# A retention layer's recurrence products as three products of rounded parts, with the query decay applied on the way out of PSUM

## The chip, the cores and the metric

The kernel runs on one core of one Trainium2 chip. The metric is the device time of one execution in microseconds (us).

## The reference

A block of two layers on a sequence of 1024 rows of 1024 floats is followed by a second block; the change touches only the first layer of the first block, a retention layer with 4 heads, keys and queries of width 256 and values of width 512, in chunks of 128 rows:

```python
log_gamma = jnp.log(1.0 - 2.0 ** (-5.0 - jnp.arange(h, dtype=jnp.float32)))
idx = jnp.arange(c, dtype=jnp.float32)
intra_decay = ...  # exp((i - j) * log_gamma) where i >= j, else 0
q_decay = jnp.exp((idx + 1.0)[:, None] * log_gamma[None, :])
k_decay = jnp.exp((c - 1.0 - idx)[:, None] * log_gamma[None, :])
chunk_decay = jnp.exp(c * log_gamma)
k = k * dk ** -0.5

def step(state, inp):
    qc, kc, vc = inp
    scores = jnp.einsum('bihd,bjhd->bhij', qc, kc) * intra_decay[None]
    intra = jnp.einsum('bhij,bjhe->bihe', scores, vc)
    inter = jnp.einsum('bihd,bhde->bihe', qc, state) * q_decay[None, :, :, None]
    new_state = (state * chunk_decay[None, :, None, None]
                 + jnp.einsum('bjhd,bjhe->bhde', kc * k_decay[None, :, :, None], vc))
    return new_state, intra + inter
```

The output is then normalised by row, multiplied by silu(gate), and projected; its input is an RMS norm of x times a weight of 1024 by 6144.

## The kernel before

The work is written by hand for five engine queues; semaphores order them. `retain` is the stage in question. After the normed input stands transposed in SBUF (`hT`), a loop runs over the 4 heads. Each head has three passes over 8 tiles of 128 rows: pass 0 projects query and key (512 columns) and VectorE rotates them into `rot`; pass 1 projects the values and ScalarE copies them into `v`; pass 2 projects the gate and runs the recurrence, one chunk a tile.

Every projection (`products`, line 91) is made of three products of rounded parts: both operands are split into a high part in the type fp32r and a low part, the rest in fp32r, and high times high, low times high and high times low are summed in PSUM. A split of a matrix costs a ScalarE copy (high, line 407) and a VectorE subtraction (low, line 477). The products of the recurrence have plain fp32 operands instead.

In pass 2 TensorE does, for tile t: four transposes of `rot` (line 366) into the bank `p_tr`; the first half of the gate projection (12 products); the scores (line 372, 128 by 128); the state's update `p_kv` = decayed keys by values (line 380, two products of 512 columns, not for the last tile); the second half of the gate (12 products); the output `p_o` = masked scores by values (line 387) plus decayed queries by state (line 392, two, not for the first tile).

Around it, ScalarE copies the transposed queries and keys from `p_tr` to `qkT` (line 455), makes silu of the gate (459), issues the store of the tile before, squares the output with a row sum (465), and divides (467). GpSimd decays the keys (302) and the queries (310) and takes the root (316). VectorE masks the scores (556), updates the state once the output product of the tile is done (563, 566), and writes the gated output (573). The queues also carry the splits of the next weights, four 128x512 pieces at a time: the second half of the gate's weights at the very end of pass 1 (they need the last value projection done), the next head's first half after the fifth tile of pass 2 (t == 4), its second half after the last. On VectorE and ScalarE each instruction waits behind the one before it, and `split_next(1, 1)` is the last step of both before tile 0 of pass 2.

Of the kernel before, what the change touches and what calls it, by code (L numbers as in the profile page):

```python
# [22 lines left out]
P = 128  # L23
# [76 lines left out]
class Mem:  # L100


    def __init__(self, nc, ctx, prefix):
        self.nc, self.ctx, self.prefix = nc, ctx, prefix
        self.signals = []
        ctx.callback(self.clear_signals)

    def sb(self, name, *shape, dt=F32):
        return self.ctx.enter_context(self.nc.sbuf_tensor(f"{self.prefix}_{name}_sb", list(shape), dt))

# [73 lines left out]
def retain(nc, ident, dram, early, hT, w_first, w_second, o_dram):  # L184
# [9 lines left out]
    with ExitStack() as ctx:  # L194
# [3 lines left out]
        v = mem.sb("v", P, TILES, RET_V)  # L198
        g_col = mem.sb("g_col", P, KT)
# [7 lines left out]
        qdT = mem.sb("qdT", P, 2, 2, P)  # L207
        k_dec = mem.sb("k_dec", P, 2, RET_QK)
        gate = mem.sb("gate", P, 2, RET_V)
        scoresT = mem.sb("scoresT", P, 2, P)  # L210
        state = mem.sb("state", P, 2, RET_V)
        o_junk = mem.sb("o_junk", P, RET_V)
# [12 lines left out]
        row_factors = [scoresT[:, b, :] for b in range(2)]  # L225
# [16 lines left out]
        (qkT_tr, qkT_copied, s_done, masked, kdec_done, qdT_done, kv_done, state_done, o_done) = mem.sems(  # L242
            "qkT_tr", "qkT_copied", "s_done", "masked", "kdec_done", "qdT_done", "kv_done", "state_done", "o_done")
# [7 lines left out]
        def block_number(head, c, per, plus):  # L251

            return head.times(PASSES * per, c * per + plus)

# [30 lines left out]
        def _(pool):  # L285
# [8 lines left out]
            with pool.Fori(0, RET_HEADS) as h:  # L294
                head = Place(h, 1, 0)

                def decay_keys(t):

                    pool.wait_ge(rot_done, head.times(TILES, t + 1))
                    if t >= 2:  # L300
                        pool.wait_ge(kv_done, head.times(2 * (TILES - 1), 2 * (t - 1)))
                    pool.tensor_tensor(k_dec[:, t % 2, :], rot[:, t, RET_QK:], k_decay.broadcast_to([P, RET_QK]), ALU.mult).then_inc(kdec_done, 1)

                pool.wait_ge(tab_in, head.times(16, 16))
                decay_keys(0)
                for t in range(TILES):
                    if t >= 1:

                        pool.wait_ge(qkT_copied, head.times(TILES, t + 1))
                        pool.tensor_tensor(qdT[:, t % 2], qkT[:, t % 2, 0:2, :],  # L310
                                           q_decay.rearrange("p (a n) -> p a n", a=1).broadcast_to([P, 2, P]), ALU.mult).then_inc(qdT_done, 1)
                    if t + 1 < TILES - 1:
# [2490 lines left out]
```

## Time and profile before

| | |
|---|---|
| median of three runs | 2470.94 us (2467.70 to 2477.11) |
| the profiled execution | 2472.37 us |
| its span in the profile | 2470.6 us |
| granted TensorE clock, mean | 0.973 |
| TensorE busy (matmuls) | 2320.0 us, 94% |
| VectorE, ScalarE, GpSimd busy | 1020.8, 827.5, 237.6 us |
| the four passes 2 | about 82 us each, from about 132, 291.5, 451 and 610.5 us |

The profiled execution's own time is 1.8 us over the span. A matmul's length in the profile covers its way through the array, and lengths overlap; what a matmul costs in a row of them is the distance between two starts. PE is TensorE, PEld its weight loads, DVE VectorE, ACT ScalarE, POOL GpSimd. In a timeline "x4" is four instructions merged, and a number in brackets is the idle time before, with what ended it.

### The profile page before, as it was taken

Reading aid. Unit: us, or ns where it says so; the run is one execution under the profiler, and the core shown is the slowest. Engines: PE = TensorE matmul, PEld = TensorE weight load, DVE = VectorE, ACT = ScalarE, POOL = GpSimd, SP = SyncE. Lnnn points to the kernel's source line nnn. Section 1 sums busy time; section 2 is a strip of 40 time slices with the busy share of each in tenths; the row PEclk is TensorE's granted clock in tenths of the full one; section 3 lists DMA queues with packets and bytes.
Section 4 is the critical chain, followed back from the end, with each engine's and each line's share of the span. In section 5 each row is a group of like instructions: output and inputs, shape, how many; then the busy total and the mean of one; then the engine's idle time right before and its main releaser. Section 6 shows DMA issues by size and latency. Waiting matters only on the chain. (4 is left out here: it accounts for less than half of the span.)

```text
span 2470.6 us, 33196 instructions
## 1 busy us (share of the span) xinstructions
PE 2320.0 (94%) x11754; PEld 1812.7 (73%) x11754; DVE 1020.8 (41%) x2882; ACT 827.5 (33%) x2132; POOL 237.6 (10%) x371
## 2 busy tenths in 40 slices
PE   6999999999979997999989799989999999699998
PEld 5877867768758886677767686767777677688876
DVE  4323224123224114355443325666565666533342
ACT  4121221221223113455543224544444544423232
POOL 1010010010010000122110000010010100101013
PEclk9999999999989998999999899999999999899999
DMA  3111111111126113011133501110111102333322
GB/s 139 37 51 51 59 49 49 55 42 57 42 93 239 68 60 128 7 50 50 48 107 112 180 14 58 58 42 23 44 43 60 41 9 75 93 107 112 102 94 86
DMA packets 125301, 175.12 MB, mean 71 GB/s; under 512 B 7577, under 2 KB 73177, under 8 KB 123617
## 3 DMA queue, kind: packets, MB, share of 16 engines
q1 hardware_dynamic: 119088, 157.39, 18.9%
q10 hardware_dynamic: 6064, 15.84, 1.7%
q8 instruction: 82, 1.34, 0.2%
q14 instruction: 67, 0.54, 0.1%
HBM read 143.79 MB, written 29.42 MB: 70 GB/s over the span
## 5 line engine op out<-in xcount | busy, mean ns | idle before, releaser
L91 PE MATMUL heads_p_ps<-ret_w_second_hi_sb,ret_hT_hi_sb 128*128 128x512 f32 x384 | 161.6, 421 | 0.0
L91 PE MATMUL heads_p_ps<-ret_w_second_lo_sb,ret_hT_hi_sb 128*128 128x512 f32 x384 | 149.9, 390 | 0.0
L91 PE MATMUL heads_p_ps<-ret_w_second_hi_sb,ret_hT_lo_sb 128*128 128x512 f32 x384 | 149.4, 389 | 0.0
L91 PE MATMUL att_proj_ps<-br_w_second_hi_sb,br_hT_hi_sb 128*128 128x512 f32 x272 | 117.2, 431 | 2.9 <-DVE br_w_second_lo_sb L2096 2.9
L91 PE MATMUL att_proj_ps<-br_w_second_lo_sb,br_hT_hi_sb 128*128 128x512 f32 x272 | 106.9, 393 | 0.0
L91 PE MATMUL att_proj_ps<-br_w_second_hi_sb,br_hT_lo_sb 128*128 128x512 f32 x272 | 106.5, 392 | 0.0
L2056 ACT ACTIVATE br_x_sb<-br_x_sb,att_max_neg_sb 128x256 f32<-128x256 f32 (+7 forms) x128 | 97.8, 767 | 15.5 <-DVE att_max_neg_sb L2269 15.4
L566 DVE SCALAR_TENSOR_TENSOR heads_state_sb<-heads_state_sb,heads_tab_sb,heads_kv_ps 128x512 f32<-128x512 f32 x48 | 33.7, 744 | 161.0 <-PE heads_o_ps L392 161.0
L91 PEld LDWEIGHTS heads_p_ps<-ret_w_second_hi_sb,ret_hT_lo_sb 128*128 128x128 f32 x384 | 72.2, 188 | 20.9 <-issue 6.7
L91 PEld LDWEIGHTS heads_p_ps<-ret_w_second_hi_sb,ret_hT_hi_sb 128*128 128x128 f32 x384 | 72.1, 188 | 20.6 <-issue 6.7
L459 ACT ACTIVATE heads_gate_sb<-heads_p_ps 128x512 f32<-128x512 f32 x32 | 19.1, 597 | 196.4 <-PE heads_p_ps L91 196.4
L91 PEld LDWEIGHTS heads_p_ps<-ret_w_second_lo_sb,ret_hT_hi_sb 128*128 128x128 f32 x384 | 72.1, 188 | 15.7
L2466 PE MATMUL mrg_b_ps<-mrg_w_br_hi_sb,mrg_yT_hi_sb 128*128 128x256 f32 x256 | 74.0, 289 | 9.2 <-DVE mrg_w_br_lo_sb L2627 8.1
L2535 ACT ACTIVATE mrg_yT_hi_sb<-br_y_raw_sb 128x1024 fp32r<-128x1024 f32 x32 | 33.9, 1060 | 140.1 <-PE mrg_b_ps L2466 119.9
L91 PE MATMUL swa_p_ps<-swa_w_first_hi_sb,swa_hT_hi_sb 128*128 128x512 f32 x160 | 70.5, 441 | 10.5 <-DVE swa_qn_sb L1352 7.0
L91 PE MATMUL att_proj_ps<-br_w_fox_hi_sb,br_hT_hi_sb 128*128 128x512 f32 x144 | 64.9, 451 | 12.1 <-ACT att_vz_fox_sb L1953 8.8
L1886 PEld LDWEIGHTS att_t_ps<-all_ident_sb,br_x_sb 128*128 128x128 f32 x432 | 48.1, 142 | 37.0 <-issue 24.0
L2466 PE MATMUL mrg_b_ps<-mrg_w_br_lo_sb,mrg_yT_hi_sb 128*128 128x256 f32 x256 | 73.0, 285 | 0.0
L2466 PE MATMUL mrg_b_ps<-mrg_w_br_hi_sb,mrg_yT_lo_sb 128*128 128x256 f32 x256 | 73.0, 285 | 0.0
L1886 PE MATMUL att_t_ps<-all_ident_sb,br_x_sb 128*128 128x128 f32 x432 | 69.2, 286 | 3.8 <-DVE br_x_sb L2284 1.9
L407 ACT ACTIVATE ret_w_second_hi_sb<-early_w_kv_sb 128x512 fp32r<-128x512 f32 x52 | 28.5, 620 | 126.8 <-PE heads_p_ps L91 126.8
L2649 DVE TENSOR_TENSOR mrg_sig_sb<-mrg_b_ps,mrg_sig_sb 128x512 f32<-128x512 f32 x32 | 22.0, 689 | 112.3 <-PE mrg_b_ps L2466 112.3
(448 smaller groups left out, 6274.3 us busy)
## 6 DMA issues: line engine op xcount, KB each, us to landing
early_w_kv_sb<-a_w_blocks SPq DMA_DIRECT2D x28, 1024.0 KB, 5.4
all_w_block_sb<-w_turns SPq DMA_DIRECT2D x12, 2048.0 KB, 9.4
br_y_raw_sb<-branch_yT_dram SPq DMA_DIRECT2D x32, 512.0 KB, 4.2
ret_o_dram<-early_x_rows_sb ACTq DMA_DIRECT2D x32, 256.0 KB, 2.4
all_w_block_sb<-swa_turns SPq DMA_DIRECT2D x4, 2048.0 KB, 10.0
ret_out_o_rows_sb<-ret_o_dram ACTq DMA_DIRECT2D x6, 1024.0 KB, 5.2
x_dram<-early_x_rows_sb SPq DMA_DIRECT2D x12, 512.0 KB, 3.3
heads_v_sb<-x SPq DMA_DIRECT2D x8, 512.0 KB, 4.1
```

Source lines behind the costliest of these rows:

```text
L91: mm = pe.matmul(out, rows[a], w[b], start=(k == 0 and a + b == 0), stop=(k == KT - 1 and b == 1))
L407: act.activation(w_at(kind)(k)[0], w_raw[:, k % HALF, :], ACT.Copy).then_inc(w_hi, 1)
L459: act.activation(gate[:, b, :], p_proj[b][:], ACT.Silu).then_inc(gate_done, 1)
L566: dve.scalar_tensor_tensor(state[:, k, :], state[:, k, :], chunk_decay, p_kv[k][:], ALU.mult, ALU.add).then_inc(state_done, 1)
L1886: tr = pe.transpose(p_tr[b][:, j * P:(j + 1) * P], probs[:, t % 2, a, (lo + j) * P:(lo + j + 1) * P], ident[:])
L2056: act.activation(part, part, ACT.Exp, bias=max_neg[:, t % 2, a:a + 1], scale=SCALE, accum_out=p_sum[:, t % 2, a:a + 1]).then_inc(exp_done, 1)
L2466: mm = pe.matmul(p_br[b][:, n * QW:(n + 1) * QW], rows[i], w[j], start=(k + i + j == 0), stop=(k == PAIRS - 1 and j == 1))
L2535: act.activation(y_parts[t % 2][0][:], y_raw[:, t % RAWS], ACT.Copy).then_inc(y_hi, 1)
L2649: dve.tensor_tensor(sig[:, t % 2, :], p_br[t % 2][:], sig[:, t % 2, :], ALU.mult).then_inc(prod_done, 1)
```

## The change

All products of the recurrence with 512 columns are made of three products of rounded parts (`three`). For this the values, the decayed keys, the decayed queries, the masked scores and the state are split: the high part on ScalarE (`value_high`, `key_high`, `state_high`, the query copy), the low part on VectorE; the high part of the scores is VectorE's too, by a second masking. GpSimd keeps only the root. The transposed queries go to the bank `p_s` beside the scores, and VectorE multiplies them by the decay as it takes them out (`decay_queries`); the scores are made of the decayed queries, and the table that masks them takes that decay out again. ScalarE copies only the keys. The state's update no longer waits for the tile's output product, since that product reads the parts and not the state; it waits for ScalarE's copy of the state's high part. The scores remain fp32 products. The low part of the values lies over the values.

```diff
+        v_low = mem.over("v", "v_low", P, TILES, RET_V, dt=F32R)
+        v_high = mem.sb("v_high", P, 2, RET_V, dt=F32R)
...
+        def three(pe, out, rows, w, first, last):
+
+            for a, b in ((0, 0), (1, 0), (0, 1)):
+                mm = pe.matmul(out, rows[a], w[b], start=first and a + b == 0, stop=last and b == 1)
+            return mm
...
-                pe.wait_ge(qkT_copied, head.times(TILES, t + 1))
+                pe.wait_ge(kT_copied, head.times(TILES, t + 1))
+                pe.wait_ge(qd_done, head.times(TILES, t + 1))
...
+                    pe.wait_ge(v_lo, head.times(TILES, t + 1))
                     if t < TILES - 1:
-                        pe.wait_ge(kdec_done, head.times(TILES - 1, t + 1))
+                        pe.wait_ge(kd_lo, head.times(TILES - 1, t + 1))
...
                         for k in range(2):
-                            pe.matmul(p_kv[k][:], k_dec[:, b, k * P:(k + 1) * P], v[:, t, :],
-                                      start=True, stop=True).then_inc(kv_done, 1)
+                            three(pe, p_kv[k][:], [part[:, b, k * P:(k + 1) * P] for part in k_dec], v_parts(t),
+                                  True, True).then_inc(kv_done, 1)
...
-                    pe.wait_ge(masked, head.times(TILES, t + 1))
+                    pe.wait_ge(sc_lo, head.times(TILES, t + 1))
...
-                    mm = pe.matmul(p_o[b][:], scoresT[:, b, :], v[:, t, :], start=True, stop=(t == 0))
+                    mm = three(pe, p_o[b][:], [part[:, b, :] for part in scoresT], v_parts(t), True, t == 0)
                     if t >= 1:
-                        pe.wait_ge(qdT_done, head.times(TILES - 1, t))
-                        pe.wait_ge(state_done, head.times(2 * (TILES - 1), 2 * t))
+                        pe.wait_ge(qd_lo, head.times(TILES - 1, t))
+                        pe.wait_ge(st_lo, head.times(2 * (TILES - 1), 2 * t))
                         for k in range(2):
-                            mm = pe.matmul(p_o[b][:], qdT[:, b, k, :], state[:, k, :], start=False, stop=(k == 1))
+                            mm = three(pe, p_o[b][:], [part[:, b, k, :] for part in qdT], [part[:, k, :] for part in state_parts],
+                                       False, k == 1)
...
+                act.wait_ge(tab_in, head.times(16, 16))
+                value_high(0)
+                key_high(0)
                 split_next(1, 1)
                 for t in range(TILES):
                     b = t % 2
                     act.wait_ge(qkT_tr, head.times(TILES, t + 1))
-                    act.activation(qkT[:, b], p_tr[:].rearrange("p (k n) -> p k n", k=4), ACT.Copy).then_inc(qkT_copied, 1)
+                    act.activation(qkT[:, b, 2:4], p_tr[:, 2 * P:4 * P].rearrange("p (k n) -> p k n", k=2), ACT.Copy).then_inc(kT_copied, 1)
+                    if t >= 1:
+                        act.wait_ge(qd_done, head.times(TILES, t + 1))
+                        act.activation(qdT[0][:, b], qkT[:, b, 0:2], ACT.Copy).then_inc(qd_hi, 1)
+                    if t + 1 < TILES:
+                        value_high(t + 1)
+                    if t + 1 < TILES - 1:
+                        key_high(t + 1)
...
                     act.activation(o_ms[:, b:b + 1], o_ssq[:, b:b + 1], ACT.Copy, scale=1.0 / RET_V, bias=EPS).then_inc(oms_done, 1)
+                    if t < TILES - 1:
+                        state_high(t)
...
                 split_next(0, 1)
                 split_next(1, 0)
+                dve.wait_ge(tab_in, head.times(16, 16))
+                value_low(0)
+                key_low(0)
                 split_next(1, 1)
-                dve.wait_ge(tab_in, head.times(16, 16))
+                decay_queries(0)
                 for t in range(TILES):
                     b = t % 2
 
+                    if t >= 1:
+                        dve.wait_ge(qd_hi, head.times(TILES - 1, t))
+                        dve.tensor_tensor(qdT[1][:, b], qkT[:, b, 0:2], full(qdT[0])[:, b], ALU.subtract).then_inc(qd_lo, 1)
                     dve.wait_ge(s_done, head.times(TILES, t + 1))
...
+                    if t + 1 < TILES:
+                        value_low(t + 1)
+                    if t + 1 < TILES - 1:
+                        key_low(t + 1)
 
                     if t < TILES - 1:
-                        dve.wait_ge(o_done, head.times(TILES, t + 1))
...
+                        decay_queries(t + 1)
+                        for k in range(2):
+                            dve.wait_ge(st_hi, head.times(2 * (TILES - 1), 2 * t + k + 1))
+                            dve.tensor_tensor(state_parts[1][:, k, :], state[:, k, :], full(state_parts[0])[:, k, :], ALU.subtract).then_inc(st_lo, 1)
```

On VectorE, at the start of pass 2 before the change (line 477 with `second` is the low half of the gate's last weights, 556 the first masking; register rows stand between):

```order
106 L477 TENSOR_TENSOR ret_w_second_lo_sb<-early_w_kv_sb,ret_w_second_hi_sb 128x512 [waits heads_w_hi]
107 L528 REGISTER_ALU
108 L477 TENSOR_TENSOR ret_w_second_lo_sb<-early_w_kv_sb,ret_w_second_hi_sb 128x512 [waits heads_w_hi]
109 L528 REGISTER_ALU
110 L477 TENSOR_TENSOR ret_w_second_lo_sb<-early_w_kv_sb,ret_w_second_hi_sb 128x512 [waits heads_w_hi]
111 L528 REGISTER_ALU
112 L477 TENSOR_TENSOR ret_w_second_lo_sb<-early_w_kv_sb,ret_w_second_hi_sb 128x512 [waits heads_w_hi]
113 L556 TENSOR_TENSOR heads_scoresT_sb<-heads_s_ps,heads_tab_sb 128x128 [waits heads_s_done,heads_tab_in]
```

The same place on VectorE with the change:

```order
105 L588 TENSOR_TENSOR heads_v_low_sb<-heads_v_sb,heads_v_high_sb 128x512 [waits heads_v_hi,heads_tab_in]
106 L592 ISA
107 L593 SCALAR_TENSOR_TENSOR heads_k_dec_lo_sb<-all_w_block_sb,heads_tab_sb,heads_k_dec_hi_sb 128x256 [waits heads_kd_hi]
108 L565 REGISTER_ALU
109 L514 TENSOR_TENSOR ret_w_second_lo_sb<-early_w_kv_sb,ret_w_second_hi_sb 128x512 [waits heads_w_hi]
110 L565 REGISTER_ALU
111 L514 TENSOR_TENSOR ret_w_second_lo_sb<-early_w_kv_sb,ret_w_second_hi_sb 128x512 [waits heads_w_hi]
112 L565 REGISTER_ALU
113 L514 TENSOR_TENSOR ret_w_second_lo_sb<-early_w_kv_sb,ret_w_second_hi_sb 128x512 [waits heads_w_hi]
114 L565 REGISTER_ALU
115 L514 TENSOR_TENSOR ret_w_second_lo_sb<-early_w_kv_sb,ret_w_second_hi_sb 128x512 [waits heads_w_hi]
116 L599 TENSOR_TENSOR heads_qkT_sb<-heads_s_ps,heads_tab_sb 128x256 [waits heads_qkT_tr]
```

Two subtractions stand ahead of the four of the weights now, and the decay of the first queries, for which TensorE's scores wait, stands behind them.

On ScalarE, inside pass 2 (second tile) before the change (the squares of one tile, then the copy of the next tile's transposes):

```order
62 L465 ACTIVATE heads_o_junk_sb,heads_o_ssq_sb<-heads_o_ps 128x512 [waits heads_o_done]
63 L467 ACTIVATE heads_o_ms_sb<-heads_o_ssq_sb 128x1 [waits heads_o_sq]
64 L455 ACTIVATE heads_qkT_sb<-heads_tr_ps 128x512 [waits heads_qkT_tr]
65 L459 ACTIVATE heads_gate_sb<-heads_p_ps 128x512 [waits heads_g_done]
66 L442 ISA [waits heads_gated]
67 L442 DMA ret_o_dram<-early_x_rows_sb 128x512
```

And with the change:

```order
67 L500 ACTIVATE heads_by_sin_sb,heads_o_ssq_sb<-heads_o_ps 128x512 [waits heads_o_done]
68 L502 ACTIVATE heads_o_ms_sb<-heads_o_ssq_sb 128x1 [waits heads_o_sq]
69 L466 ISA
70 L467 ACTIVATE heads_state_hi_sb<-heads_state_sb 128x512 [waits heads_state_done]
71 L466 REGISTER_ALU
72 L467 ACTIVATE heads_state_hi_sb<-heads_state_sb 128x512 [waits heads_state_done]
73 L483 ACTIVATE heads_qkT_sb<-heads_tr_ps 128x256 [waits heads_qkT_tr]
74 L486 ACTIVATE heads_qdT_hi_sb<-heads_qkT_sb 128x256 [waits heads_qd_done]
75 L454 ACTIVATE heads_v_high_sb<-heads_v_sb 128x512 [waits heads_v_copied]
76 L461 ACTIVATE heads_k_dec_hi_sb<-all_w_block_sb,heads_tab_sb 128x256 [waits heads_kv_done,heads_rot_done]
77 L494 ACTIVATE heads_gate_sb<-heads_p_ps 128x512 [waits heads_g_done]
```

Two copies of the state have come between the division and the copy of the keys, and three copies behind that one.

## Rows read from the trace of the kernel before

**Rows 1.** The page: span, and TensorE's busy time, share and instructions.

```profile
span 2470.6 us, 33196 instructions
PE 2320.0 (94%) x11754; PEld 1812.7 (73%) x11754; DVE 1020.8 (41%) x2882; ACT 827.5 (33%) x2132; POOL 237.6 (10%) x371
```

**Rows 2.** Busy time by stretch: the columns, and pass 2 of head 0.

```profile
core 0: us, PE busy (x) PEld busy (x) DVE busy (x) ACT busy (x) POOL busy (x), PEclk, DMA share, GB/s
132.00:214.00 82.00, 81.93 (x330) 56.23 (x329) 22.21 (x37) 20.85 (x47) 11.63 (x19) 1.00 0.13 49
```

**Rows 3.** Groups by line: the fp32 products of the recurrence.

```profile
L380 PE MATMUL heads_kv_ps<-heads_v_sb,heads_k_dec_sb 128*128 128x512 f32 x112 | 52.7, 593 | 0.0
L392 PE MATMUL heads_o_ps<-heads_state_sb,heads_qdT_sb 128*128 128x512 f32 x112 | 52.6, 592 | 0.0
...
L387 PE MATMUL heads_o_ps<-heads_v_sb,heads_scoresT_sb 128*128 128x512 f32 x64 | 32.6, 592 | 0.0
```

**Rows 4.** Timeline, one tile of pass 2: start, length, engine, operation, [idle before].

```profile
194.79 0.60 PE L366 MATMUL heads_tr_ps<-all_ident_sb,all_w_block_sb 128*128 128x128 f32 x4
...
197.96 0.61 PE L372 MATMUL heads_s_ps<-heads_qkT_sb 128*128 128x128 f32 x4
...
203.75 1.88 PE L392 MATMUL heads_o_ps<-heads_state_sb,heads_qdT_sb 128*128 128x512 f32 x4
...
205.46 0.60 PE L366 MATMUL heads_tr_ps<-all_ident_sb,all_w_block_sb 128*128 128x128 f32 x4
...
205.66 0.60 ACT L465 ACTIVATE heads_o_junk_sb<-heads_o_ps 128x512 f32<-128x512 f32 x1 [1.98 <-PE heads_o_ps L392]
...
206.49 0.58 ACT L455 ACTIVATE heads_qkT_sb<-heads_tr_ps 128x512 f32<-128x512 f32 x1
```

**Rows 5.** Timeline, TensorE: 93 starts of pass 0, then 11 of pass 2.

```profile
215.10 0.40 PE L91 MATMUL heads_p_ps<-ret_w_qk_hi_sb,ret_hT_hi_sb 128*128 128x512 f32 x1
...
235.97 0.39 PE L91 MATMUL heads_p_ps<-ret_w_second_lo_sb,ret_hT_hi_sb 128*128 128x512 f32 x1
...
138.01 0.40 PE L91 MATMUL heads_p_ps<-ret_w_second_hi_sb,ret_hT_lo_sb 128*128 128x512 f32 x1
...
140.30 0.39 PE L91 MATMUL heads_p_ps<-ret_w_second_lo_sb,ret_hT_hi_sb 128*128 128x512 f32 x1
```

**Rows 6.** Timeline at the start of pass 2, head 0.

```profile
132.10 0.60 PE L366 MATMUL heads_tr_ps<-all_ident_sb,all_w_block_sb 128*128 128x128 f32 x4
...
132.79 2.19 ACT L407 ACTIVATE ret_w_second_hi_sb<-early_w_kv_sb 128x512 fp32r<-128x512 f32 x4
...
133.45 2.50 DVE L477 TENSOR_TENSOR ret_w_second_lo_sb<-early_w_kv_sb,ret_w_second_hi_sb 128x512 fp32r<-128x512 f32 x4 [11.11 <-ACT ret_w_second_hi_sb L407]
...
134.87 0.59 ACT L455 ACTIVATE heads_qkT_sb<-heads_tr_ps 128x512 f32<-128x512 f32 x1
...
135.51 0.52 PEld L372 LDWEIGHTS heads_s_ps<-heads_qkT_sb 128*128 128x128 f32 x4 [0.49 <-ACT heads_qkT_sb L455]
```

**Rows 7.** Groups by line: shorter VectorE operations of this stage.

```profile
L541 DVE TENSOR_TENSOR all_w_block_sb<-all_w_block_sb,heads_by_sin_sb 128x256 f32<-128x256 f32 x32 | 13.6, 426 | 1.1
...
L556 DVE TENSOR_TENSOR heads_scoresT_sb<-heads_s_ps,heads_tab_sb 128x128 f32<-128x128 f32 x32 | 9.3, 290 | 31.8 <-PE heads_s_ps L372 31.8
```

**Rows 8.** Timeline of ScalarE and VectorE around the fifth and sixth tile, head 0.

```profile
182.23 2.18 ACT L407 ACTIVATE ret_w_qk_hi_sb<-early_w_kv_sb 128x512 fp32r<-128x512 f32 x4
...
186.82 2.66 DVE L477 TENSOR_TENSOR ret_w_qk_lo_sb<-early_w_kv_sb,ret_w_qk_hi_sb 128x512 fp32r<-128x512 f32 x4
```

**Rows 9.** Timeline: two later gaps of TensorE; by stretch: the clock after each.

```profile
1629.50 0.50 PE L91 MATMUL att_proj_ps<-br_w_fox_hi_sb,br_hT_hi_sb 128*128 128x512 f32 x1 [2.39 <-ACT att_vz_fox_sb L1953]
...
1720.46 0.49 PE L1868 MATMUL att_s_ps<-att_qkT_diff_sb 64*128 64x128 f32 x4 [2.08 <-issue]
...
1720.50:1724.00 3.50, 3.50 (x16) 3.09 (x17) 2.77 (x11) 3.33 (x8) 0.00 (x0) 0.56 0.03 9
1629.50:1633.00 3.50, 3.50 (x17) 2.94 (x18) 3.50 (x11) 0.96 (x3) 0.00 (x0) 1.00 0.00 0
```

More of the change, by code:

```diff
@@ L104, in __init__, with over @@
         self.nc, self.ctx, self.prefix = nc, ctx, prefix
-        self.signals = []
+        self.signals, self.at = [], {}
         ctx.callback(self.clear_signals)
     def sb(self, name, *shape, dt=F32):
+        self.at[name] = -(-self.nc.sbuf_base // 32) * 32
         return self.ctx.enter_context(self.nc.sbuf_tensor(f"{self.prefix}_{name}_sb", list(shape), dt))
+    def over(self, under, name, *shape, dt=F32):
+        return self.nc.alloc_sbuf_tensor_at(f"{self.prefix}_{name}_sb", list(shape), dt, offset=self.at[under])
     def parts(self, name, *shape):
@@ L224, in retain @@
         sq_junk = o_gated.rearrange("p b n -> p (b n)")
-        row_factors = [scoresT[:, b, :] for b in range(2)]
+        row_factors = [qkT[:, 0, b, :] for b in range(2)]
         onehot, rel = gate[0:REL_BUCKETS, 0, 0:EXT], gate[0:REL_BUCKETS, 1, 0:SWA_HEADS]
@@ L295, in _ @@
                 head = Place(h, 1, 0)
[L297 to L305, printed above, removed]
-                for t in range(TILES):
[L307 to L312, printed above, removed]
-                        decay_keys(t + 1)
+                for t in range(TILES):
                     pool.wait_ge(oms_done, head.times(TILES, t + 1))
@@ L442, in store_rows, with value_high, key_high, state_high @@
                     act.dma_start(o_dram[t * P:(t + 1) * P, bass.ds(head.times(RET_V), RET_V)], o_gated[:, t % 2, :]).then_inc(o_out[t % 2], 16)
+                def value_high(t):
+                    act.wait_ge(v_copied, head.times(TILES, t + 1))
+                    act.activation(v_high[:, t % 2, :], v[:, t, :], ACT.Copy).then_inc(v_hi, 1)
+                def key_high(t):
+                    act.wait_ge(rot_done, head.times(TILES, t + 1))
+                    if t >= 2:
+                        act.wait_ge(kv_done, head.times(2 * (TILES - 1), 2 * (t - 1)))
+                    act.activation(k_dec[0][:, t % 2, :], rot[:, t, RET_QK:], ACT.Copy, scale=k_decay).then_inc(kd_hi, 1)
+                def state_high(t):
+                    for k in range(2):
+                        act.wait_ge(state_done, head.times(2 * (TILES - 1), 2 * t + k + 1))
+                        act.activation(state_parts[0][:, k, :], state[:, k, :], ACT.Copy).then_inc(st_hi, 1)
                 split_next(0, 0)
@@ L547, in _, with value_low, key_low @@
                         split_next(0, 0)
+                def value_low(t):
+                    dve.wait_ge(v_hi, head.times(TILES, t + 1))
+                    dve.tensor_tensor(v_low[:, t, :], v[:, t, :], full(v_high)[:, t % 2, :], ALU.subtract).then_inc(v_lo, 1)
+                def key_low(t):
+                    dve.wait_ge(kd_hi, head.times(TILES - 1, t + 1))
+                    dve.scalar_tensor_tensor(k_dec[1][:, t % 2, :], rot[:, t, RET_QK:], k_decay, full(k_dec[0])[:, t % 2, :],
+                                             ALU.mult, ALU.subtract).then_inc(kd_lo, 1)
```

35 lines of the change are left out of this document (26 added, 9 removed).

## The prediction

> **What bounds the kernel now.** I read the page first: TensorE has matmuls in flight for 94% of the span [rows 1]. The busy times by stretch then show the stage that the change touches, pass 2 of the loop over heads: 81.93 of 82 us busy, with the clock at 1.00, that is 2.4 GHz, while VectorE and ScalarE work a quarter of the time each and GpSimd a seventh [rows 2]. The other three heads have the same pass. So every microsecond that TensorE's queue loses or gains in these four passes is one of the kernel's, as long as nothing it waits for comes late. The reader should then look at the distance between starts in the timeline, and at what each engine does ahead of TensorE's waits.
>
> **The gain.** The fp32 products of 512 columns show as 112, 112 and 64 instructions, two for each product in the program, so 144 products [rows 3] (by the program: four heads, 14 for the state, 8 and 14 for the output). Four such instructions last from 203.75 to the transposes at 205.46 [rows 4]: 0.4275 us each, 0.855 a product. A product of rounded parts starts every (235.97 - 215.10) / 92 = 0.2268 us in pass 0 and (140.30 - 138.01) / 10 = 0.2290 in pass 2 [rows 5]. Three at 0.228 make 0.684 us, so a product gains 0.171 us and 144 gain 24.6 us; the two spacings give 24.2 and 25.2. The type, the shape and the source are those of the rows, so I take no wider bounds. The Trainium skill (TensorE: Matmul & The Clock Gate, "Wait — 56ns, not 53.3ns?") states N / 2.4 GHz + 2.5 ns from start to start of a warm matmul, 215.7 ns at 512 columns; an estimate by it is a gain of 30 us. The trace has 0.227 and more, and I go by the trace.
>
> The transposes, the scores and the gate's projections keep their number and shape on TensorE. The scores' two waits instead of one cost nothing when both are met. In a full tile TensorE goes from 10.67 us [rows 4] to about 9.8.
>
> **Start of pass 2, in every head.** Here is the cost. TensorE is at the scores 3.17 us after the tile's first transpose (197.96 - 194.79) [rows 4]; in head 0 that would be 135.27, and it begins at 135.51, since ScalarE's copy comes 0.24 us late [rows 6]. ScalarE starts a 128x512 split every 0.52 us ((134.87 - 132.79) / 4), VectorE one every 0.625 (2.50 / 4) [rows 6]. With the change ScalarE makes the high parts of values and keys first, at 132.79 and 133.31. VectorE can take the low part of the values at 133.45 and needs 0.625; that of the keys starts at 134.07 and takes 0.42 for 256 columns [rows 7]; then come the four subtractions of the weights to 134.5 + 2.5 = 137.0, and only then the decay of the queries, again 0.42 us, with some 0.05 until TensorE sees it. ScalarE's high parts are always ahead of this. TensorE starts the scores at 137.45 instead of 135.51: 1.9 us later, 7.7 us in four heads. Nothing hides it: TensorE runs in order and the products behind the scores wait with it. The lower bound is that both added subtractions are cheap (1.3 us a head, 5 in all), the upper that all of ScalarE's and VectorE's added work came in series (0.52 + 0.4 + 0.625 + 0.42 + 0.42, 2.4 us a head, 9.6 in all); the row of VectorE's spacing is the nearest, so I stay at 1.9.
>
> **The clock after that stall.** Such a stall is about 2.1 us of nothing on TensorE. A gap of 2.08 us in a later stage is followed by 0.56 of the clock over 3.5 us, which is 1.5 us of work lost; a gap of 2.39 us is followed by 1.00 [rows 9]. So it happens to some and not to others. I price it at 1.6 us and take it for one in three of the four stalls, because the work before and behind them is dense: 2.1 us, between 0 and 6.4. The Trainium skill (the same page, "Why this matters for your kernels") advises about idle gaps in such a way that a stall this short would leave the clock alone. By it the forecast would lie 2.1 us lower; the gap of 2.08 us speaks against it.
>
> **Inside the pass.** ScalarE comes first. It is done with the squares 1.03 us after the next tile's first transpose (206.49 - 205.46) [rows 4]. Then come two state copies (1.04) and the copy of the keys, 0.58 for twice the columns [rows 4], so at most 0.4 here: done at 2.5, and the scores are due at 3.17. Margin 0.7. The state is updated long before, since it waits for the output product no more. VectorE: the decay of the queries at 0.6 to 1.0; low parts of the state when the copies are there, to 2.95; the gated output to 3.7; low queries to 4.1; then the scores' three operations of 0.29 [rows 7], to 5.0. TensorE asks for them at 3.17 + 0.44 + 1.37 + 2.75, that is 7.7. Values, keys and state follow to 7.6, and the next decay waits for the next transposes. VectorE is busy about 6 us in 9.8, so it is not the bound. GpSimd loses its two decays, off the path.
>
> One tile in eight is tighter: the sixth, when the next head's weights are split. ScalarE's four high parts [rows 8] end about 0.6 us after the transposes instead of at their start, because the tile has become shorter by 0.87 and the splits not; the copy of the keys then lands at about 3.3, so 0.15 late. VectorE's four subtractions of 2.66 us in all [rows 8] start behind the gated output, at 4.6, and end at 7.2; low queries and scores end at 8.4 where TensorE, itself 0.15 late, wants them at 7.9. Together 0.5 to 0.6 us; 0.45 if VectorE keeps the 0.625 of the rows once GpSimd is quiet. I take 0.45, 1.8 us in four heads, between 0 and 4.
>
> The end of a head is the same chain as before (squares, root, gated output, four splits), as far behind TensorE as before. The bank, the store queue, the weights' loads and the later layers are untouched; SP's load that waits for the last subtraction starts 1 us later, forty us ahead of its use. The row factors before the loop have another place and the same size: nothing.
>
> **Sum:** -24.6 + 7.7 + 2.1 + 1.8 = -13.0 us. The sum is made against the profiled execution, 2472.37 us (span 2470.6 and 1.8 around it), so 2459.4; against the median of the runs shown, 2470.9, it gives 2457.9, and that is my number. A measurement of this kernel can tell about 0.5%, or 12.4 us, from no change; the bound is 2458.6.
>
> **The rivals.** (1) The stall and the clock: the start of pass 2 costs 2.4 us a head and the clock halves after each stall, the sixth tile costs 0.9: -24.6 + 9.6 + 6.4 + 3.6 = -5.0, 2466. For it: a gap of 2.08 us was enough once [rows 9]. Against it: the longer gap that was not. (2) The stall is smaller than I think, since VectorE's short operations overlap and the clock stays: -24.6 + 5 + 0 + 0.6 = -19, 2452. (3) Slower than before: ScalarE's two state copies in front of the copy of the keys are late in every tile. The margin is 0.7 us, and from there each microsecond is 28 us, on 28 tiles of four heads. If writing the state's parts, or VectorE's update that waits for the copy of the tile before, holds ScalarE for 1.8 us more than I count, the loss is 1.1 us a tile, 31 us, and the time 2489; it passes the old one at 0.46 us a tile. Only then does it decide. Against it: ScalarE's split rows show 0.52 us with the same output type, and the update has 3 us to spare. (4) The change does not do what it says: products with freshly made low parts go no faster than the fp32 ones. Then only the costs stand, +8 us or so, 2480. Rows 5 speak against it in two places.
>
> **How the numbers follow.** My forecast has 0.60, with a range of its own from 2453 to 2463; it straddles the bound, and I give 0.38 to the part under it. Rival 1 has 0.20, rival 2 0.11, rival 3 0.06, rival 4 0.03. Faster by over 0.5%: 0.38 + 0.11 = 0.49. Within 0.5%: 0.22 + 0.20 + 0.03 = 0.45. Slower: 0.06. The range that should hold it 8 times in 10 goes from rival 2 to a bit over rival 1: 2451 to 2468.
>
> **What would show it.** Four passes of about 79 us; 432 instructions of 512 columns where there were 288, starting every 0.227 to 0.229 us; the scores of each head's first tile with some 2 us of idle time before them, ended by VectorE's decay of the queries; a stretch or two at half clock behind them; a small wait in the sixth tile and none in the others. The prediction is wrong if the copy of the keys or the parts of the scores end idle time in most tiles, if that first stall is under 1 or over 3 us, or if the spacing is not that of rows 5.

## The result, and the profile after

The change takes **2460.78 us** (median of six runs, 2458.4 to 2462.62) where the kernel before takes 2474.25 in the runs beside it (six, 2467.7 to 2477.11). The ratio is 0.9948, with a 95% interval of 0.9937 to 0.9959. By the ratio that is 12.9 us less of 2474.25 (the two medians are 13.5 apart), against a forecast of 13.0. The profiled execution took 2458.4 us, its span is 2456.6.

The page of the changed kernel:

```profile
span 2456.6 us, 33964 instructions
...
PE 2297.0 (94%) x11898; PEld 1836.7 (75%) x11898; DVE 1116.2 (45%) x3122; ACT 886.5 (36%) x2276; POOL 202.8 (8%) x315
```

TensorE has 144 instructions more and is in flight 23 us less than in [rows 1]. VectorE, at 1116.2 us, has 95 more than before, ScalarE 59 more.

Busy time by stretch, over the whole span: up to the first transposes of head 0, from there to the end of the last pass 2, and the rest (columns as in [rows 2]). The changed kernel, then the last two stretches of the kernel before:

```profile
core 0: us, PE busy (x) PEld busy (x) DVE busy (x) ACT busy (x) POOL busy (x), PEclk, DMA share, GB/s
0.00:132.27 132.27, 110.50 (x515) 92.38 (x516) 50.07 (x85) 34.37 (x53) 6.23 (x21) 0.96 0.26 90
132.27:712.85 580.58, 571.36 (x2609) 469.69 (x2607) 266.44 (x535) 187.34 (x413) 17.06 (x31) 0.99 0.15 51
712.85:2456.60 1743.75, 1615.13 (x8777) 1274.62 (x8776) 799.67 (x2502) 664.75 (x1810) 179.46 (x263) 0.97 0.23 77
```

```profile
132.10:724.54 592.44, 591.13 (x2465) 441.27 (x2463) 169.88 (x295) 128.29 (x269) 51.72 (x85) 1.00 0.13 50
724.54:2470.60 1746.06, 1617.20 (x8777) 1277.48 (x8776) 800.78 (x2502) 664.88 (x1810) 178.48 (x263) 0.96 0.23 77
```

The stretch that holds the four passes 2 went from 592.44 to 580.58 us, 11.9 less, and there the 144 added instructions stand. TensorE no longer fills it: 571.36 of 580.58, where it was 591.13 of 592.44. The third stretch has the same instructions in both kernels and came out 2.3 us shorter, the first 0.2 longer. The third is no part of the change: with this kernel it lasted 1743.75 here and 1749.9 in a later profiled execution of it (2462.9 of span, the last pass over at 713.02). So a single profiled execution says nothing below some 6 us, and passes are compared one by one from here on.

One thing to correct first: the table above has the passes 2 at 132, 291.5, 451 and 610.5 us. The trace before has the first transposes of the four heads at 132.1, 302.2, 472.2 and 642.2. The passes' length of 82 us is right, and no number of the prediction hangs on those starts.

Pass 2 of head 0 by busy time, to set beside [rows 2]:

```profile
132.00:214.00 82.00, 79.95 (x380) 65.69 (x380) 47.88 (x100) 38.55 (x90) 4.40 (x8) 1.00 0.14 49
```

VectorE went from 22 to 48 us, ScalarE from 21 to 39, GpSimd from 12 to 4. A product now shows as three instructions where [rows 3] had two. In the groups by line, the high-by-high one of each kind:

```profile
L269 PE MATMUL heads_kv_ps<-heads_v_high_sb,heads_k_dec_hi_sb 128*128 128x512 f32 x56 | 25.3, 452 | 0.0
...
L269 PE MATMUL heads_o_ps<-heads_state_hi_sb,heads_qdT_hi_sb 128*128 128x512 f32 x56 | 22.0, 393 | 0.0
...
L269 PE MATMUL heads_o_ps<-heads_v_high_sb,heads_scoresT_hi_sb 128*128 128x512 f32 x32 | 12.7, 397 | 0.0
```

Each kind stands in three forms (high by high, high by low, low by high), and one form stands 56 + 56 + 32 = 144 times.

The timeline at the start of pass 2, head 0, against [rows 6]:

```profile
132.27 0.38 PE L370 MATMUL heads_s_ps<-all_ident_sb,all_w_block_sb 128*128 128x128 f32 x2
...
132.96 0.62 ACT L454 ACTIVATE heads_v_high_sb<-heads_v_sb 128x512 fp32r<-128x512 f32 x1
...
133.48 0.50 ACT L461 ACTIVATE heads_k_dec_hi_sb<-all_w_block_sb,heads_tab_sb 128x256 fp32r<-128x256 f32 x1
...
133.68 0.69 DVE L588 TENSOR_TENSOR heads_v_low_sb<-heads_v_sb,heads_v_high_sb 128x512 fp32r<-128x512 f32 x1 [11.18 <-ACT heads_v_high_sb L454]
...
134.29 0.48 DVE L593 SCALAR_TENSOR_TENSOR heads_k_dec_lo_sb<-all_w_block_sb,heads_tab_sb,heads_k_dec_hi_sb 128x256 fp32r<-128x256 f32 x1
...
134.69 2.49 DVE L514 TENSOR_TENSOR ret_w_second_lo_sb<-early_w_kv_sb,ret_w_second_hi_sb 128x512 fp32r<-128x512 f32 x4
...
135.96 0.37 ACT L483 ACTIVATE heads_qkT_sb<-heads_tr_ps 128x256 f32<-128x256 f32 x1
...
137.10 0.42 DVE L599 TENSOR_TENSOR heads_qkT_sb<-heads_s_ps,heads_tab_sb 128x256 f32<-128x256 f32 x1
...
137.66 0.68 PE L377 MATMUL heads_s_ps<-heads_qkT_sb 128*128 128x128 f32 x4 [2.05 <-DVE heads_qkT_sb L599]
```

TensorE now waits 2.05 us for the decay of the queries, which stands behind six subtractions on VectorE. It reaches the scores 5.39 us after the first transposes, where it took 3.41. The chain is the one foretold: 133.68, 134.29, 134.69, 137.10, against 133.45, 134.07, 134.5, 137.0. In all four heads (waits of TensorE, from 45 to 730 us: sum, times, longest):

```profile
PE heads_s_ps L377 <- DVE heads_qkT_sb L599: 8.2, 4, 2.1
```

And the stretches of 3.4 us behind these four stalls:

```profile
138.00:141.40 3.40, 3.40 (x18) 2.81 (x17) 2.91 (x7) 0.55 (x1) 0.00 (x0) 1.00 0.79 228
304.70:308.10 3.40, 3.40 (x10) 2.62 (x9) 2.94 (x7) 0.11 (x1) 0.00 (x0) 0.50 0.87 237
472.00:475.40 3.40, 3.40 (x11) 2.82 (x11) 2.36 (x6) 0.69 (x1) 0.00 (x0) 0.51 0.74 222
639.70:643.10 3.40, 3.40 (x17) 2.88 (x18) 2.62 (x7) 0.84 (x1) 0.00 (x0) 1.00 0.68 210
```

The granted clock was 0.50 and 0.51 behind the stalls of heads 1 and 2, that is 1.2 GHz, and 1.00 behind those of heads 0 and 3. The first tile took 10.75 us from transpose to transpose in head 0 and 12.31 in head 1: so such a fall of the clock ("a fall" from here on) costs 1.6 us.

Inside the pass, first the second tile of head 0:

```profile
145.09 0.36 ACT L483 ACTIVATE heads_qkT_sb<-heads_tr_ps 128x256 f32<-128x256 f32 x1
...
146.21 0.61 PE L377 MATMUL heads_s_ps<-heads_qkT_sb 128*128 128x128 f32 x4
```

The same view later in head 0:

```profile
172.68 0.38 PE L370 MATMUL heads_s_ps<-all_ident_sb,all_w_block_sb 128*128 128x128 f32 x2
...
175.89 0.61 PE L377 MATMUL heads_s_ps<-heads_qkT_sb 128*128 128x128 f32 x4
...
180.49 0.40 PE L269 MATMUL heads_o_ps<-heads_v_high_sb,heads_scoresT_hi_sb 128*128 128x512 f32 x1
...
181.66 0.39 PE L269 MATMUL heads_o_ps<-heads_state_lo_sb,heads_qdT_hi_sb 128*128 128x512 f32 x1
...
182.57 0.38 PE L370 MATMUL heads_s_ps<-all_ident_sb,all_w_block_sb 128*128 128x128 f32 x2
...
186.60 2.49 DVE L514 TENSOR_TENSOR ret_w_qk_lo_sb<-early_w_kv_sb,ret_w_qk_hi_sb 128x512 fp32r<-128x512 f32 x4
...
189.93 0.29 DVE L620 TENSOR_TENSOR heads_scoresT_lo_sb<-heads_masked_rows_sb,heads_scoresT_hi_sb 128x128 fp32r<-128x128 f32 x1
...
190.39 0.39 PE L269 MATMUL heads_o_ps<-heads_v_high_sb,heads_scoresT_hi_sb 128*128 128x512 f32 x1
```

A full tile lasts 182.57 - 172.68 = 9.89 us where it lasted 10.67 [rows 4]. The copy of the keys is done at 145.45, 0.76 us ahead of the scores. The sixth tile (from 182.57) loses nothing: its low part of the scores is done at 190.22, TensorE takes it at 190.39, and the tile's period is 9.90.

### The profile page after: what moved, and what is told of

The parts are those of the page before. It is cut to its first block and busy times, and to the rows that moved or that the text cites. A ratio compares the mean times of both kernels' runs of the same rounds, so it can differ in the third digit from the quotient of the medians.

```text
span 2456.6 us, 33964 instructions
## 1 busy us (share of the span) xinstructions
PE 2297.0 (94%) x11898; PEld 1836.7 (75%) x11898; DVE 1116.2 (45%) x3122; ACT 886.5 (36%) x2276; POOL 202.8 (8%) x315
## 5 line engine op out<-in xcount | busy, mean ns | idle before, releaser
L91 PE MATMUL heads_p_ps<-ret_w_second_hi_sb,ret_hT_hi_sb 128*128 128x512 f32 x384 | 150.6, 392 | 0.0
L2128 ACT ACTIVATE br_x_sb<-br_x_sb,att_max_neg_sb 128x256 f32<-128x256 f32 (+7 forms) x128 | 97.8, 767 | 13.1 <-DVE att_max_neg_sb L2341 12.9
L319 POOL TENSOR_TENSOR heads_o_rstd_sb<-heads_o_ms_sb,heads_minus_half_sb 128x1 f32<-128x1 f32 x32 | 17.6, 550 | 656.3 <-ACT heads_o_ms_sb L502 656.3
L840 DVE TENSOR_TENSOR early_x_rows_sb<-ret_out_y_ps,early_x_rows_sb 128x512 f32<-128x512 f32 x16 | 10.9, 688 | 133.5 <-PE ret_out_y_ps L767 133.5
```

The lines of the kernel that those rows point to most:

```text
L91: mm = pe.matmul(out, rows[a], w[b], start=(k == 0 and a + b == 0), stop=(k == KT - 1 and b == 1))
L319: pool.tensor_tensor(o_rstd[:, t % 2:t % 2 + 1], o_ms[:, t % 2:t % 2 + 1], minus_half[:], ALU.pow).then_inc(orstd_done, 1)
L840: dve.tensor_tensor(x_rows[:, t % 2, cols], p_y[t % 2][half][:], x_rows[:, t % 2, cols], ALU.add).then_inc(x_added, 1)
L2128: act.activation(part, part, ACT.Exp, bias=max_neg[:, t % 2, a:a + 1], scale=SCALE, accum_out=p_sum[:, t % 2, a:a + 1]).then_inc(exp_done, 1)
```

## The experiments

Every run is set beside runs of the kernel before on the same chip. "Pass" is the time from the first transposes of a head to the start of its last product.

**1. The changed kernel again**, with no edit: does the halved clock belong to heads 1 and 2?

> The change itself once more, as the yardstick for the kernels run beside it. Theory 1 (the stall at the first scores of each head is VectorE's queue, and the clock falls after some of these stalls by chance of phase): about 2461 us, 2.05 us idle before each head's first scores, and half clock behind none to four of the four. Theory 2 (the clock falls in heads 1 and 2 because of something in those heads): half clock again behind heads 1 and 2, and only there.

2459.49 us, ratio 0.9945 (0.9932 to 0.9959). The same stall of 2.05 us in each head, the same periods to 0.01 us, and falls again in heads 1 and 2 of the profiled execution.

> The change a third time, for its trace. Theory 4: the same four stalls of 2.05 us, and half clock behind another set of them if the run's start lies otherwise; if heads 1 and 2 are special, half clock behind these two again.

One execution, 2458.80 us, on another chip: here they came in heads 0, 2 and 3 (first tiles of 12.30, 10.74, 12.30 and 12.32 us). So no head is bound to a fall; a stall in the same place is followed by one in one execution and by none in another. The chip does not decide alone either, since the four equal stalls of one execution end both ways.

**2. The decay of the queries ahead of the splits of the weights, on VectorE alone:**

```diff
                 value_low(0)
                 key_low(0)
-                split_next(1, 1)
                 decay_queries(0)
+                split_next(1, 1)
```

> Only the decay of the first queries is moved ahead of the last four weight subtractions on VectorE; ScalarE's order is that of the change. Theory 1: VectorE is no longer late, but ScalarE's copy of the keys ends 135.96 + 0.37 = 136.33 in head 0, 1.06 us after the scores could start; so about 0.9 to 1.1 us idle before the first scores, ended by ScalarE, no fall of the clock, 4 x 1.0 + 3.2 = 7 us less than the change, 2454. If VectorE alone were to blame: no stall, 2450.

2453.95 us, 0.9919 (0.9904 to 0.9934). TensorE's wait, in the view of waits, is shorter, and another ends it:

```profile
PE heads_s_ps L377 <- ACT heads_qkT_sb L483: 3.1, 4, 0.8
```

It is now ScalarE's copy of the keys, 0.8 us. The pass lasts 77.08 us against 78.35 without a fall, and the clock falls behind none of the four stalls.

**3. The first high parts of values and keys earlier, on ScalarE alone**, while the last values are still copied:

```diff
                     if t == 4:
                         split_next(1, 0)
-                act.wait_ge(tab_in, head.times(16, 16))
-                value_high(0)
-                key_high(0)
+                    if t == 5:
+                        act.wait_ge(tab_in, head.times(16, 16))
+                        value_high(0)
+                        key_high(0)
                 split_next(1, 1)
```

> Only the high parts of the first values and keys are moved, into pass 1 after the sixth value copy; VectorE's order is that of the change. Theory 1: the four subtractions start 0.65 us behind the split on ScalarE and end 3.85 us after the first transpose, the decay 0.45 later, so 1.1 us idle before the first scores, ended by VectorE, no fall of the clock, 4 x 0.95 + 3.2 = 7 us less than the change, 2454. If the two added subtractions were the whole of it: less than 0.3 us, 2450.

2454.67 us, 0.9917 (0.9901 to 0.9932), pass 77.27, no fall:

```profile
PE heads_s_ps L377 <- DVE heads_qkT_sb L600: 3.9, 4, 1.0
```

VectorE still ends the wait, 1.0 us of it: the low parts come earlier, and the decay with them, but still behind four splits. So the stall has two causes in a row, ScalarE's order and VectorE's.

**4. Both moves together.**

> The high parts of the first values and keys are made in pass 1 after the sixth value copy, and the decay of the first queries stands ahead of the last four weight subtractions. Theory 1 (the order on VectorE and ScalarE at the start of pass 2 is the whole stall, and the stall is what lets the clock fall): less than 0.3 us idle before the first scores of each head, no half clock inside the four passes, and 4 x 2.05 + 2 x 1.6 = 11 us less than the change, about 2450. Theory 2 (the stall is ended by the decay of the queries only in name; the wait is on PSUM or on the transposes): idle time stays near 2 us and the time near 2461. Theory 3 (the clock falls whatever the stall): 2461 - 8 = 2453 and half clock still in two passes.

**2450.54 us, 0.9906 (0.9891 to 0.9922)**, by the ratio 23.3 us less than the kernel before (24.3 by the medians), and 9 us less than the change beside it, at 2459.49. The start of pass 2, head 0, by the timeline:

```profile
131.91 0.38 PE L370 MATMUL heads_s_ps<-all_ident_sb,all_w_block_sb 128*128 128x128 f32 x2
...
132.54 0.42 DVE L600 TENSOR_TENSOR heads_qkT_sb<-heads_s_ps,heads_tab_sb 128x256 f32<-128x256 f32 x1 [9.01 <-PE heads_tr_ps L370]
...
133.26 2.50 DVE L515 TENSOR_TENSOR ret_w_second_lo_sb<-early_w_kv_sb,ret_w_second_hi_sb 128x512 fp32r<-128x512 f32 x4 [0.29 <-ACT ret_w_second_hi_sb L414]
...
134.68 0.37 ACT L484 ACTIVATE heads_qkT_sb<-heads_tr_ps 128x256 f32<-128x256 f32 x1
...
135.10 0.52 PEld L377 LDWEIGHTS heads_s_ps<-heads_qkT_sb 128*128 128x128 f32 x4 [0.28 <-ACT heads_qkT_sb L484]
```

The decay is made 0.63 us after the first transposes, and the subtractions of the weights come behind it. TensorE is at the scores 3.19 us after the first transposes. The 0.28 us in brackets is idle time of the weight loads; the matmuls lose nothing by it, since in a full tile, where nothing waits, the distance is 3.21 (172.68 to 175.89 in the changed kernel). The first tile takes 8.60 us (before 9.29), the pass 76.20, no fall in any head. From the first transposes of a head to the start of the projection's product behind its last one it is 76.43 against 82.31 before: 5.88 us, 23.5 in four heads. What the change lost at the start of pass 2, it lost by the order of work alone.

**5. The products in fp32 again, everything else as changed.** This kernel makes every split and leaves the low parts out of the products:

```diff
-            for a, b in ((0, 0), (1, 0), (0, 1)):
-                mm = pe.matmul(out, rows[a], w[b], start=first and a + b == 0, stop=last and b == 1)
-            return mm
+            return pe.matmul(out, rows[0].bitcast(F32), w[0].bitcast(F32), start=first, stop=last)
```

> All splits, waits and orders of the change, but each product of the recurrence is one plain fp32 product of the two high parts, as before (its low parts are made and left out of the product). Theory 1: it loses what the products gave, 23 to 25 us against the change, about 2484 to 2486, so 10 us over the kernel before, which is the price of the splits alone. A rival by which the products gain less than their spacing says and the rest comes from the state's update that waits for less: 2465 to 2475. On the spacing: if the busier ScalarE and VectorE are what stretches the matmuls of pass 2 from 0.229 to 0.231-0.233 us, the gate's products in this kernel have 0.231 too; if it is the new products, 0.229.

2487.46 us, 1.0051 (1.0037 to 1.0065): all of the cost, none of the gain. Its tiles from the third on take 10.67 us, exactly as before, so in tiles of that length the splits on ScalarE and VectorE cost TensorE nothing. The same stall is there:

TensorE's waits for the decay, and then the four stretches behind the stalls:

```profile
PE heads_s_ps L375 <- DVE heads_qkT_sb L597: 8.2, 4, 2.1
```

```profile
137.80:141.20 3.40, 3.40 (x9) 1.85 (x8) 2.38 (x6) 0.65 (x1) 0.00 (x0) 0.50 0.63 237
311.90:315.30 3.40, 3.40 (x6) 1.34 (x5) 2.38 (x6) 0.25 (x1) 0.00 (x0) 0.50 0.79 292
485.90:489.30 3.40, 3.40 (x6) 1.69 (x5) 2.74 (x7) 0.00 (x0) 0.00 (x0) 0.51 0.83 302
660.00:663.40 3.40, 3.40 (x7) 1.96 (x6) 2.58 (x5) 0.00 (x0) 0.00 (x0) 0.50 0.83 295
```

This time the clock fell in all four heads. To price the terms one needs a pass without a fall:

> The fp32 products with all splits a second time, for its trace: the same four stalls of 2.05 us. Theory 4: the heads are 173.7 us apart, and the falls may be other than four of four. If fp32 products let the clock fall more easily than products of parts: four of four again.

It took 2484.71 us (one execution) and has two passes without one (heads 0 and 3, pass 83.85; before, 81.88). Timeline of TensorE in head 0: first transposes, and the second product of the projection behind the pass. Then that last row of the changed kernel and of the kernel before:

```profile
132.04 0.38 PE L368 MATMUL heads_s_ps<-all_ident_sb,all_w_block_sb 128*128 128x128 f32 x2
...
216.55 0.40 PE L91 MATMUL heads_p_ps<-ret_w_qk_hi_sb,ret_hT_lo_sb 128*128 128x512 f32 x1
```

```profile
211.07 0.40 PE L91 MATMUL heads_p_ps<-ret_w_qk_hi_sb,ret_hT_lo_sb 128*128 128x512 f32 x1
```

```profile
214.64 0.40 PE L91 MATMUL heads_p_ps<-ret_w_qk_hi_sb,ret_hT_lo_sb 128*128 128x512 f32 x1
```

From the first transposes that is 84.51 us with fp32 products, 211.07 - 132.27 = 78.80 with parts, 214.64 - 132.10 = 82.54 before. So the products gain 5.71 us a head, **22.8** in four; the splits cost 1.97 a head, **7.9** in four, all at the start of the pass.

**6. A longer stall.** One more subtraction of 512 columns ahead of the first decay, into a buffer that nobody reads:

```diff
                 split_next(1, 1)
+                dve.tensor_tensor(spare[:], sin[:, 0:4, :].rearrange("p t n -> p (t n)"), full(v_high)[:, 0, :], ALU.subtract).then_inc(again, 1)
+                dve.wait_ge(again, head.times(1, 1))
                 decay_queries(0)
```

> One more 128x512 subtraction into a spare tile stands before the decay of the first queries on VectorE, and is waited for. Theory 1: 2.05 + 0.7 = 2.75 us idle before each head's first scores, and the clock falls behind three or four of them instead of two: 4 x 0.7 + 1 to 2 falls of 1.6 = 4.4 to 6 us over the change, about 2466. If the clock does not depend on the stall's length: 2.8 us, 2464, with two falls.

2461.14 us, 0.9951 (0.9936 to 0.9966). The stall is 2.8 us and the clock fell once, in head 0:

```profile
PE heads_s_ps L379 <- DVE heads_qkT_sb L601: 11.1, 4, 2.8
```

```profile
137.80:141.20 3.40, 2.88 (x9) 2.52 (x10) 1.92 (x6) 0.68 (x1) 0.00 (x0) 0.50 0.71 232
306.00:309.40 3.40, 2.74 (x14) 2.37 (x15) 2.39 (x8) 0.82 (x1) 0.00 (x0) 1.00 0.61 224
473.00:476.40 3.40, 2.74 (x14) 2.37 (x15) 2.40 (x8) 0.82 (x1) 0.00 (x0) 1.00 0.67 203
640.00:643.40 3.40, 2.71 (x14) 2.34 (x15) 2.40 (x8) 0.85 (x1) 0.00 (x0) 1.00 0.58 207
```

> The kernel with the longer stall (2.75 us) a second time, for its trace: one fall of four the first time. Theory 4: zero to four, by where the stalls lie; if the length alone decided, one of four would have been chance and three or four come now.

One execution, 2455.24 us: no fall in four. With 0.73 us more of waiting in every head the kernel still measures like the change. In the profiled executions it has fewer falls (a fall here costs 12.78 - 11.48 = 1.3 us of the first tile), and my expectation that a longer stall falls at least as often is not met in them. But the profiled execution of the first four was the quickest, 2455.51 us beside 2460.49 to 2464.07, and how many falls the other three had is not known: the 1 in 8 may be too low, and that fewer falls make up for the longer stall is argued, not shown.

**7. A middle one**: experiments 3 and 6 together.

> The high parts of the first values and keys are made in pass 1, and the spare subtraction stands before the decay of the first queries: a stall between those of a3 (1.0 us) and of the change (2.05 us), about 1.7 us. Theory 4 (a stall lets the clock fall by where in time it lies, and the more easily the longer it is, but not below some length near 2 us): no half clock inside the four passes, a ratio between those of a3 and of the change, about 2457. If chance alone decides at any length: one or two falls.

```profile
PE heads_s_ps L379 <- DVE heads_qkT_sb L602: 6.8, 4, 1.7
```

1.7 us, no fall in four heads; 2454.94 us, 0.9925 (0.9908 to 0.9941), pass 78.0.

**8. The decay left to GpSimd**, as before the change, with the products of parts and their splits as changed: four transposes into one bank, ScalarE copies queries and keys together, makes the high part of the queries behind those of values and keys instead of ahead of them, and the old table for the mask.

```diff
+                    if t >= 1:
+                        pool.wait_ge(kT_copied, head.times(TILES, t + 1))
+                        pool.tensor_tensor(qd_full[:, t % 2], qkT[:, t % 2, 0:2, :],
+                                           q_decay.rearrange("p (a n) -> p a n", a=1).broadcast_to([P, 2, P]), ALU.mult).then_inc(qd_done, 1)
...
-                    pe.wait_ge(qd_done, head.times(TILES, t + 1))
...
-                    act.activation(qkT[:, b, 2:4], p_tr[:, 2 * P:4 * P].rearrange("p (k n) -> p k n", k=2), ACT.Copy).then_inc(kT_copied, 1)
+                    act.activation(qkT[:, b], p_tr[:].rearrange("p (k n) -> p k n", k=4), ACT.Copy).then_inc(kT_copied, 1)
...
-                decay_queries(0)
...
-                        decay_queries(t + 1)
```

> The second part of the change undone: four transposes into one bank, ScalarE copies queries and keys together, the scores are made of the undecayed queries, and GpSimd decays the queries for the output product; all products of rounded parts stay. Theory 1: the first scores wait for ScalarE's copy instead of VectorE's decay, which ends at 135.96 + 0.58 = 136.54 in head 0, so 1.1 to 1.2 us idle; no fall of the clock; nothing late in the other tiles; 4 x 0.85 + 3.2 = 6.6 us less than the change, 2454. A rival by which taking the decay off GpSimd is worth something inside the pass (GpSimd's 0.74 us ahead of the root and of the low queries): the tile grows from 9.89, by 0.1 us or more, and the time is that of the change or over.

2457.29 us, 0.9926 (0.9913 to 0.9940), between the change and experiment 4:

```profile
PE heads_s_ps L381 <- ACT heads_qkT_sb L487: 3.9, 4, 1.0
```

Nothing on TensorE waits for VectorE's six subtractions here; the copy behind ScalarE's two high parts is 1.0 us late. The sixth tile takes 9.97 us instead of 9.89. The pass lasts 77.38 us against 78.35, with no fall. In the order in which the change has it, then, the second half of the change (the decay on the way out of PSUM) takes back 1.0 us a head by the passes and makes the stall of the length that had falls behind it; by the ratios the two kernels are 0.2% apart (0.9926 and 0.9945), with intervals that overlap. In the order of experiment 4 the same decay costs none of this. Whether the GpSimd version with its copies moved would be as fast as experiment 4 was not tried.

## Why the prediction was right, and where its terms were off

It said 2457.9 us, in 2451 to 2468; the time is 2460.78. The kernel before stood at 2474.25 in the runs beside it and not at 2470.94, so the difference is the better test: 12.9 by the ratio, 13.5 by the medians, against 13.0. Three terms were off by 1 to 2 us and cancel in part. That the total agrees to a tenth is luck: the measured terms add up to 11.8, and the rest is no term of the prediction; the two stretches outside that of the passes alone came out 2.1 us shorter together, which no term foresaw.

| step | forecast | measured | from |
|---|---|---|---|
| 144 products in parts | -24.6 | -22.8 | experiment 5 |
| start of pass 2, four heads | +7.7 | +7.9 | experiment 5 |
| clock behind the stalls | +2.1 | +3.1 | two falls of 1.6 in the profiled run |
| sixth tile | +1.8 | 0 | period 9.90 |
| sum | -13.0 | -11.8 | stretches: 592.44 to 580.58, -11.9 |

- **The products.** The step that was mis-sized is "three at 0.228 make 0.684 us". The nine output products of a tile take 182.57 - 180.49 = 2.08 us, 0.231 from start to start, where six fp32 instructions of 0.4275 took 2.565: 0.162 us a product, not 0.171. Over all 144 it is 22.8 / 144 = 0.158. Within those nine the first five distances are 0.234 (181.66 - 180.49) and the last four 0.2275: the short spacing of [rows 5], 0.2268, and one longer than its 0.2290 stand side by side, and in this pass the longer has the larger share. I had taken a mean of the two rows. The gate's products grow wider too: behind the transposes at 172.68 ten distances measure 0.231 each (173.35 to 175.66). The splits that go on beside are not the cause: in experiment 5, with the same splits, only two distances behind the transposes are wide and the next eight measure 0.227 (197.83 to 199.65), as in the kernel before. What differs are the products of parts around them; why the row is wider beside them is open. An estimate by the 215.7 ns of the Trainium skill (TensorE: Matmul & The Clock Gate, "Wait — 56ns, not 53.3ns?") is a gain of 30 us. This trace does not agree: no ten distances in a row have a mean under 0.2266.
- **The start of pass 2.** Right by mechanism and by size: 1.97 us a head for 1.9, the wait ended by VectorE's decay of the queries. Experiments 2 to 4 take the stall apart as the prediction built it up.
- **The clock.** I said one in three of four stalls, at 1.6 us each. Over five profiled executions with this very stall (the change three times, experiment 5 twice) the clock fell behind 13 of 20, 2.6 of four. A fall cost 1.56 to 1.7 us in them, so the term was 4.2 us on the average (3.7 by the three of the change alone, 7 of 12) and 3.1 in the profiled one. The gap of 2.08 us of [rows 9] had a fall behind it; now thirteen stalls of 2.05 have one. The advice of the Trainium skill on idle gaps (the same page, "Why this matters for your kernels"), by which a gap this short would leave the clock alone, is not borne out here: stalls of 2.05 us had the half clock behind them 13 times in 20.
- **The sixth tile.** The step that failed is "VectorE's four subtractions start behind the gated output, at 4.6". They started 4.03 us after the transposes and took 2.49 us, so the low parts were there 0.2 us before TensorE asked. The prediction let the weights' splits on ScalarE shift all that follows by 0.8 to 0.9 us (the copy of the keys from 2.5 to 3.3, the end of the gated output from 3.7 to 4.6). The copies of the state began 1.51 us after the transposes instead of 1.03 in the fifth tile, 0.5 later: the tile is 0.78 us shorter, but the four splits also begin 0.29 earlier in theirs (8.50 us after its transposes, before 8.79). So the copy of the keys was done at 2.91, ahead of the scores. And the 2.66 us of [rows 8] is head 0 alone; in the other three heads of the kernel before the four took 2.84.
- **Inside the pass.** ScalarE ahead of the scores by 0.76 us, foretold 0.7; tile 9.89, foretold about 9.8 (at 0.231 it is 9.89). So rival 3, which needed 0.46 us a tile, had nothing.
- **The rivals.** Rival 4 is refuted by experiment 5: with fp32 products the kernel is 1% slower than the change, above the kernel before. Rival 1 had the falls nearer (in the third profiled execution of the change three of four), but neither its 2.4 us at the start of a head nor its sixth tile. Rival 2, a smaller stall and no fall, is no case of this kernel; a better order gives both (experiments 2 to 4, 2454.67 to 2450.54 us against its 2452).

The runs also show what I took for given: that the stall had to be there. "Nothing hides it" is true of the order as written only; two moved pieces of it give 2450.5 us.

## What to carry to other kernels

When work is added to helper engines that are mostly idle, look at where it stands in each queue at the start of a stage and not at their busy share: here the splits at the start of a pass, ahead of one short operation, ate a third of what 144 faster products gained (7.9 of 22.8 us), and two moves, that operation ahead of four subtractions and two high parts into the pass before, gave 9 us back. Price a product by the distance of starts in the very stretch that it will stand in, not by a mean with another. And a stall of TensorE of about 2 us is to be priced with the clock that may halve behind it, which depends on more than its length.

## What the runs showed of the hardware that was not expected

- The granted clock was half (0.50 or 0.51 in the stretches shown) behind 13 of 20 stalls of 2.05 us, behind 1 of 8 stalls of 2.78 us, and behind none of 16 stalls of 0.8 to 1.7 us. The long one had been expected to be the worst. The same kernel gave falls in heads 1 and 2 twice and in heads 0, 2 and 3 once, so neither the length of the stall nor the head decides alone. What else does stays open.
- Products of the same kind and shape do not start evenly. In the tile from 172.68 of the changed kernel the mean distance is 0.231 us for the ten behind the transposes (173.35 to 175.66), 0.232 for twelve behind the scores (176.57 to 179.36), then 0.227 for five (to 180.49), and wide again, 0.234 for five (to 181.66), at the output products, though these follow twelve products of the same shape.
- VectorE's four subtractions of the sixth tile took 2.66 us before in head 0, with an operation of GpSimd running into them (186.52 for 0.61 us, the subtractions from 186.82), and 2.84 in the other three heads, where the operation reached 0.5 us into them (head 1: 356.60 for 0.62, the subtractions from 356.73). The whole excess is in the first of the four, 0.86 and 1.03 us long instead of 0.68. They took 2.49 after, without such an operation. In experiment 8, where GpSimd decays the queries again but is done as they begin (185.14 for 0.84, the subtractions from 185.96), they also took 2.49.
